# Two transitions of a residual layer: the second norm's root taken from three sums instead of from the updated x

## The reference, cut to what matters

```python
def rmsnorm_2(x, g):
    y = x * lax.rsqrt(jnp.mean(x * x, axis=-1, keepdims=True) + NORM_EPS)
    return y * g

# per layer l; y is what the mixer's last product (conv_out_w or attn_o_w) gives
x = x + g_m[:, None, :] * rmsnorm_2(y, norm_g[l, 1])
h = modulate(rmsnorm_2(x, norm_g[l, 2]), sh_f, sc_f)      # h * (1 + scale) + shift
y = squared_relu_mlp(h, mlp_up_w[l], mlp_down_w[l])
x = x + g_f[:, None, :] * rmsnorm_2(y, norm_g[l, 3])
```

## Time and profile before

| | |
|---|---|
| median of 3 runs | 1802.6 us (1801.67 to 1802.96) |
| the profiled execution | 1802.32 us, its span 1800.5 us |
| PE busy | 1771.8 us of the span (98%) |
| DVE busy | 1069.8 us (59%) |
| ACT busy | 614.2 us (34%) |
| POOL busy | 80.4 us (4%) |
| moved | 215.85 MB, 120 GB/s |

### The profile page before, as it was taken

One profiled execution on the slowest core, in us unless ns is written; L12 is line 12 of the kernel. 1 busy time (PEld: TensorE's weight loads), 2 busy tenths in 40 slices (PEclk: granted clock), 3 DMA queues, 4 the chain that ended last, 5 costly groups with the idle time before them and its releaser, 6 DMA issues. The chain is left out here.

```text
span 1800.5 us, 22782 instructions
## 1 busy us (share of the span) xinstructions
PE 1771.8 (98%) x8216; PEld 1427.2 (79%) x8216; DVE 1069.8 (59%) x1553; ACT 614.2 (34%) x951; POOL 80.4 (4%) x133
## 2 busy tenths in 40 slices
PE   9999999999999999999999999999999999999996
PEld 7777677888888888887888888877767788888885
DVE  5586555655555576776656565657776655434354
ACT  4226444322222343223414232425344342323230
POOL 0000000000000000001000010010000100000001
PEclk9999999999999999999999999999999999999998
DMA  6231112444454434552355555521321134323221
GB/s 230 81 107 36 48 48 60 156 159 152 140 173 146 142 100 132 184 188 94 94 185 181 206 190 184 182 75 59 106 71 60 47 108 161 105 94 96 91 81 47
DMA packets 60127, 215.85 MB, mean 120 GB/s; under 512 B 6672, under 2 KB 6800, under 8 KB 59920
## 3 DMA queue, kind: packets, MB, share of 16 engines
q1 hardware_dynamic: 43632, 154.95, 25.4%
q0 software_dynamic: 16272, 59.25, 10.6%
q10 hardware_dynamic: 144, 0.59, 0.1%
HBM read 212.67 MB, written 2.10 MB: 119 GB/s over the span
## 5 line engine op out<-in xcount | busy, mean ns | idle before, releaser
L707 ACT ACTIVATE w_hi<-w_raw 128x1024 fp32r<-128x1024 f32 x285 | 300.2, 1054 | 458.8 <-PE psum L1623 416.4
L1621 PE MATMUL psum<-h_hi,w_hi 128*128 128x512 f32 x1080 | 421.3, 390 | 1.1 <-DVE h_lo L1057 0.9
L1622 PE MATMUL psum<-h_lo,w_hi 128*128 128x512 f32 x1080 | 420.2, 389 | 0.0
L1623 PE MATMUL psum<-h_hi,w_lo 128*128 128x512 f32 x1080 | 420.2, 389 | 0.0
L1030 DVE TENSOR_TENSOR w_lo<-w_raw,w_hi 128x1024 fp32r<-128x1024 f32 x285 | 348.5, 1223 | 114.1 <-ACT w_hi L707 104.1
L1621 PE MATMUL psum<-hid_hi,w_hi 128*128 128x512 f32 x760 | 295.6, 389 | 0.0
L1622 PE MATMUL psum<-hid_lo,w_hi 128*128 128x512 f32 x760 | 295.6, 389 | 0.0
L1623 PE MATMUL psum<-hid_hi,w_lo 128*128 128x512 f32 x760 | 295.6, 389 | 0.0
L1621 PEld LDWEIGHTS psum<-h_hi,w_hi 128*128 128x128 f32 x1080 | 202.7, 188 | 45.0 <-DVE h_lo L1057 1.3
L1622 PEld LDWEIGHTS psum<-h_lo,w_hi 128*128 128x128 f32 x1080 | 202.7, 188 | 42.2 <-issue 0.5
L1623 PEld LDWEIGHTS psum<-h_hi,w_lo 128*128 128x128 f32 x1080 | 202.7, 188 | 42.0
(11 more groups left out here) (274 smaller groups left out, 1906.7 us busy)
## 6 DMA issues: line engine op xcount, KB each, us to landing
w_raw<-in_wstream SPq DMA_DIRECT2D x285, 512.0 KB, 3.6
ada_raw<-in_ada POOLq DMA_DIRECT2D x112, 512.0 KB, 3.8
x<-in_xT SPq DMA_DIRECT2D x8, 256.0 KB, 6.9
outT<-x SPq DMA_DIRECT2D x8, 256.0 KB, 2.1
con<-in_consts SPq DMA_DIRECT2D x1, 1028.0 KB, 10.6
con<-in_rope ACTq DMA_DIRECT2D x1, 576.0 KB, 5.4
c_row<-in_crow POOLq DMA_DIRECT2D x1, 512.0 KB, 3.9
par<-in_params SPq DMA_DIRECT2D x1, 255.0 KB, 2.7
```

Source lines behind the costliest of these rows:

```text
L707: act.activation(w_hi[:, slot, :], w_raw[:, slot, :], ACT.Copy).then_inc(whi_done, 1)
L1621: pe.matmul(bank, w_hi[:, slot, w], hi[:, ra + k, :], start=k == 0, stop=False)
L1622: pe.matmul(bank, w_hi[:, slot, w], lo[:, ra + k, :], start=False, stop=False)
L1623: mm = pe.matmul(bank, w_lo[:, slot, w], hi[:, ra + k, :], start=False, stop=k == nk - 1)
```

## The change

The two transitions after a mixer (r_m0, r_m1) no longer use `close` and `norm`; the one after the MLP and the last update stay. Since mean(x'^2) = mean(x^2) + 2 r1 mean(x g y) + r1^2 mean((g y)^2), the second root can be had from three means that don't need r1.

- In the last product (`fore=`), after DVE's copy of a chunk to y, ACT squares y and g y, and DVE makes x g y and adds up the three. The sum of y^2 in `ss` takes chunks 0 to 6; chunk 7's squares go into the mean as a matmul of their own.
- Mean of x^2: for r_m0, ACT squares the eight chunks of x, and DVE adds them, in the last six blocks of the convolution's input product (`square_x`); for r_m1 it is the mean that the transition before had made anyway, copied by ACT into `x_mean` (`keep`). To make room, one row of `ada` moves from that stage and four from the output product to the twelve blocks in front.
- Stage `sums`: PE makes the means, then 18 short matmuls (NEW_WARM). Stage `rstd` (first): Ln, Exp, and a copy of the root to PSUM. Stage `resum`: DVE puts the mean of x'^2 together in five instructions, and begins the update. Stage `rstd` (second): Ln and Exp. Stage `renew`: DVE makes the steps r1 g y in place in y, POOL adds chunks 1 to 7 to x (DVE adds chunk 0), and DVE and ACT make h from each chunk.
- In the last step of the product ACT and DVE split one more block of weights (n+4), which the next product's first step then doesn't (`presplit=1`).

```diff
-    def close(gain, middle, end):
+    def renew(old, name, shift, inst):
+        add("sums", dict(aux=1), inst=inst)
+        rstd(EPS2, first_of=inst + 1)
+        add("resum", inst=inst, old=old)
+        rstd(EPS2, second_of=inst + 1)
+        r0 = counts["rhs"]
+        add("renew", dict(val=DT, hi=DT, rhs=DT, xup=1, xpool=DT - 1), inst=inst, old=old, gain=name, shift=shift)
+        return r0
+
+    def close(gain, middle, end, keep=False):
...
-    gemm("conv", 12, "h", h, f0=2, rows=10, scale_x=True)
-    gemm("conv", 6, "h", h, f0=6, rows=6)
+    gemm("conv", 12, "h", h, f0=2, rows=15, scale_x=True)
+    gemm("conv", 6, "h", h, f0=6, rows=5, square_x=True)
     take("g_f0", "r_f0")
-    gemm("acc", 8, "hid", hid, dst="y", first=True, sq=True, rows=4)
-    close("r_m0", 19, 15)
-    h = norm("h", gain="g_f0", shift=24)
+    gemm("acc", 8, "hid", hid, dst="y", first=True, sq=True, fore=0, old="r_m0")
+    h = renew("r_m0", "g_f0", 24, 0)
...
-            gemm("relu2", 8, "h", h, kouter=AHEAD if g == 0 else 0, rows=up[g])
+            gemm("relu2", 8, "h", h, kouter=AHEAD if g == 0 else 0, presplit=1 if g == 0 else 0, rows=up[g])
...
-    close("r_f0", 21, 16)
+    close("r_f0", 21, 16, keep=True)
...
-    gemm("acc", 8, "h", mix, dst="y", first=True, sq=True, kouter=2, begun=6,
+    gemm("acc", 8, "h", mix, dst="y", first=True, sq=True, fore=1, old="r_m1", kouter=2, begun=6,
          turn=-counts["o"] % BANKS)
-    close("r_m1", 19, 15)
-    h = norm("h", gain="g_f1", shift=88)
+    h = renew("r_m1", "g_f1", 88, 1)
...
+        root_wide, mean_g, root_new, mean_mul = psum[:, PT_BANK, :], psum[:, PT_BANK + 1, :], psum[:, PT_BANK + 1, :], psum[:, O_BANK, :]
+        def new_val(c):
+            return psum[:, (O_BANK, AUX_BANK)[c % 2], :]
...
# GpSimd
+                if s["kind"] == "renew":
+                    for c in range(1, DT):
+                        pool.wait_ge(held_done, DT * s["inst"] + c + 1)
+                        pool.tensor_tensor(x[:, c, :], x[:, c, :], y[:, c, :], ALU.add).then_inc(x_pool, 1)
...
# ScalarE, in a step of the last product
+                    if "fore" in s:
+                        c, inst = t.b, s["fore"]
+                        if c == DT - 1:
+                            n = t.n + AHEAD + 1
+                            split_hi(n // RAW + 1, n % SPLIT, t.o + 1)
...
+                        act.activation(y_sq[c % 2], y[:, c, :], ACT.Square).then_inc(y_squared, 1)
...
+                        act.activation(g_sq[c % 2], y[:, c, :], ACT.Square, scale=gain_of(s["old"], c)).then_inc(g_squared, 1)
...
+                elif kind == "rstd" and s.get("first_of"):
+                    act.wait_ge(aux_done, s["at"]["aux"])
+                    act.activation(rstd[:, :], psum[:, AUX_BANK, :], ACT.Ln, bias=eps[s["eps"]][:, :]).then_inc(ln_done, 1)
+                    act.wait_ge(ln_done, s["at"]["rstd"] + 1)
+                    act.activation(rstd[:, :], rstd[:, :], ACT.Exp, scale=-0.5).then_inc(rstd_done, 1)
+                    act.wait_ge(rstd_done, s["at"]["rstd"] + 1)
+                    act.activation(root_wide, rstd[:, :], ACT.Copy).then_inc(root_done, 1)
+                elif kind == "rstd" and s.get("second_of"):
+                    act.wait_ge(resum_done, s["second_of"])
+                    act.activation(resum, resum, ACT.Ln, bias=eps[s["eps"]][:, :]).then_inc(ln_done, 1)
+                    act.wait_ge(ln_done, s["at"]["rstd"] + 1)
+                    act.activation(root_new, resum, ACT.Exp, scale=-0.5).then_inc(rstd_done, 1)
+                elif kind == "renew":
+                    for c in range(DT):
+                        act.wait_ge(val_done, s["at"]["val"] + c + 1)
+                        act.activation(h_hi[:, c, :], new_val(c), ACT.Identity,
+                                       bias=mod[:, s["shift"] + c:s["shift"] + c + 1]).then_inc(hi_done, 1)
...
+                    if s.get("keep"):
+                        act.activation(x_mean[:, :], psum[:, AUX_BANK, :], ACT.Copy).then_inc(mean_kept, 1)
...
# VectorE, in a step of the last product (fore_sums adds y^2 and (g y)^2, add_mul adds x g y)
+                    elif evac == "acc" and "fore" in s:
+                        c, inst = t.b, s["fore"]
+                        if c >= 2:
+                            fore_sums(inst, c - 1)
+                        split_lo(t.n + AHEAD, (t.n0 + AHEAD) % SPLIT)
+                        dve.wait_ge(out_done, t.o + 1)
+                        dve.tensor_copy(y[:, c, :], bank).then_inc(bank_free, 1)
+                        dve.wait_ge(bank_free, BANKS + t.o + 1)
+                        dve.scalar_tensor_tensor(out=y_mul[c % 2], in0=y[:, c, :], scalar=gain_of(s["old"], c),
+                                                 in1=x[:, c, :], op0=ALU.mult, op1=ALU.mult).then_inc(mul_done, 1)
+                        if c >= 1:
+                            add_mul(inst, c)
+                        if c == DT - 1:
+                            n = t.n + AHEAD + 1
+                            split_lo(n, n % SPLIT)
...
+            def new_step(s, c):
+                dve.scalar_tensor_tensor(out=y[:, c, :], in0=y[:, c, :], scalar=gain_of(s["old"], c), in1=root_wide,
+                                         op0=ALU.mult, op1=ALU.mult).then_inc(held_done, 1)
+
+            def resummed(s):
+                dve.wait_ge(means_done, 3 * inst + 1)
+                dve.tensor_tensor(resum, mean_g, rstd[:, :], ALU.mult).then_inc(resum_step, 1)
...
+                dve.scalar_tensor_tensor(out=resum, in0=mean_mul, scalar=2.0, in1=resum, op0=ALU.mult, op1=ALU.add)\
+                   .then_inc(resum_step, 1)
...
+                dve.tensor_tensor(resum, resum, rstd[:, :], ALU.mult).then_inc(resum_step, 1)
...
+                    dve.tensor_tensor(resum, resum, psum[:, AUX_BANK, :], ALU.add).then_inc(resum_step, 1)
...
+                dve.tensor_scalar(resum, resum, 0.0, None, ALU.max).then_inc(resum_done, 1)
+                dve.wait_ge(root_done, inst + 1)
+                new_step(s, 0)
+                dve.wait_ge(held_done, DT * inst + 1)
+                dve.tensor_tensor(x[:, 0, :], x[:, 0, :], y[:, 0, :], ALU.add).then_inc(x_done, 1)
+                new_step(s, 1)
+
+            def renew(s):
...
+                for c in range(DT - 2):
+                    val(c)
+                    new_step(s, c + 2)
+                    low(c)
+                val(DT - 2)
+                val(DT - 1)
+                low(DT - 2)
+                low(DT - 1)
...
# TensorE
+                elif kind == "sums":
+                    pe.matmul(psum[:, AUX_BANK, :], mean[1024][:, :], ss[:, :], start=True, stop=False)
+                    pe.matmul(mean_g, mean[1024][:, :], g_sum, start=True, stop=False)
+                    pe.matmul(psum[:, AUX_BANK, :], mean[1024][:, :], y_sq[1], start=False, stop=True).then_inc(aux_done, 1)
+                    pe.matmul(mean_g, mean[1024][:, :], g_sq[1], start=False, stop=True).then_inc(means_done, 1)
+                    pe.matmul(mean_mul, mean[1024][:, :], mul_sum, start=True, stop=True).then_inc(means_done, 1)
+                    if inst == 0:
+                        pe.wait_ge(ln_done, s["at"]["rstd"] + 1)
+                        pe.matmul(psum[:, AUX_BANK, :], mean[1024][:, :], x_sum, start=True, stop=True).then_inc(means_done, 1)
+                    keep_warm(NEW_WARM, next(p for p in PLAN[idx:] if p["kind"] == "gemm")["at"]["o"] % BANKS)
```

More of the change, by code:

```diff
@@ L49 @@
 WARM_START, WARM = 28, 9
+NEW_WARM = 18
 SHIFT = 1
@@ L89, in gemm @@
         about["h0"] = hi_of[r0]
-        if evac == "acc" and about.get("sq"):
+        if evac == "acc" and about.get("sq") and "fore" not in about:
             inc.update(sqv=nblk, ss=nblk + (0 if about.get("more") else 1) - (0 if about.get("go_on") else 1))
@@ L326, in steps @@
     turns = nblk // body
-    first = 1 if stage["at"]["n"] == 0 or done else 0
+    first = 1 if stage["at"]["n"] == 0 or done or stage.get("presplit") else 0
     if last:
@@ L1094, in gemm @@
                 more = s.get("more", False)
-                if evac == "acc" and s["sq"] and not more:
+                if evac == "acc" and s["sq"] and not more and "fore" not in s:
                     dve.memset(ss[:, :], 0.0).then_inc(ss_done, 1)
@@ L1111, in step @@
                                or isinstance(t.b, int) and t.b < s.get("presplit", 0))
-                    if not nothing and not s.get("late") and not s.get("twin"):
+                    if not nothing and not s.get("late") and not s.get("twin") and "fore" not in s:
                         split_lo(t.n + AHEAD, (t.n0 + AHEAD) % SPLIT)
```

99 lines of the change are left out of this document (93 added, 6 removed).

## The result

The changed kernel takes 1792.11 us (median of 5 runs, 1791.66 to 1794.0) against 1802.6 (1801.53 to 1803.18): the ratio of the runs is 0.9946, 95% interval 0.9935 to 0.9956, so 7.9 to 11.7 us are gone. The forecast was 1793.2, range 1790.8 to 1797.2. The profiled execution has a span (first to last instruction) of 1790.3 us, 10.2 less than before.

A forecast was written before the change was run, and what follows sets the result against it. The prediction took the serial chain in two transitions, about 18.1 us each without useful PE work, as the bound. Gains of 2 x 4.68 = 9.4 us off 1802.32 gave 1792.9, or 1793.2 beside the median, range 1790.8 to 1797.2.

The forecast's parts named there:

- What bounds the kernel: Two transitions: each costs about 18.1 us in which PE makes nothing the next product needs, set by the serial chain.
- First root: In each transition, after the last copy: Ln at 2.85 us, Exp 0.71 later, DVE starts at 4.38, before 4.23.
- T: The moment at which DVE can copy the output product's last block, 834.77 us in the first transition before the change.
- Chain: DVE's mean of x'^2 and update start: dependent instructions 0.73 to 0.79 apart, first value of h at 10.22 us.
- The rule of the Trainium skill on chained Vector instructions: Semaphores cost nothing extra; by it five links are 0.6 us shorter per transition, time 1792.0; forecast followed the rows instead.
- The turn: DVE's three instructions per chunk of h, with a wait for ACT: 2.29 us a chunk, over PE's 2.04, six chunks.
- GpSimd: POOL's adds to x in the two transitions take 1.29 us each and hold up no value; nothing lost.
- Rival 1: PE's clock falls in the gap before the first chunk, then returns: 1793 to 1797, say 1795 us; chance 0.18.
- Rival 2: Lower clock stays through the next product's first chunks: each transition 10.2 us later than before, 1822 us; chance 0.05.
- Rivals 3 and 4: 3: turn longer than 2.29, 1796.6 to 1800.3 us, chance 0.08; 4: DVE late to last copy, 1797.7, chance 0.04.
- Sum: Two transitions gaining 4.68 us each, 9.4 off the profiled 1802.32: 1792.9, or 1793.2 beside the median.

The follow-up runs named there:

- kernel with the gap filled: 28 and 32 short matmuls instead of 18 in the first and third transitions, against the changed kernel; median 1793.33 us against 1792.72 on the same chip.

## Why the prediction was right, point by point

- **What bounds the kernel.** Right: 9.1 of the 10.2 us by which the spans differ lie between the last copy and the first relu of two transitions.
- **First root.** Ln came 2.86 after T (836.75; forecast 2.85), Exp 3.57 (3.56); DVE began at 4.48 (4.38). The row names PE's L2112 as what ended DVE's wait, but by the program L1402 needs only the root and the mean before it (L2110); the Exp ended at 838.09, 0.28 ahead. The other means were in time: L2112 ended at 838.36, 0.81 ahead of the second instruction, and L2116 at 839.22, 1.40 ahead of the fourth.
- **Chain.** 0.72 to 0.80 apart; I had one link of 0.79, but it is the first and not the one behind the scalar_tensor_tensor, and no run tells why. The last instruction takes 0.43 instead of 0.49. The start of two stages cost 0.39 where I had taken 0.30. First value at T + 10.31 (10.22), first matmul at 11.99 (11.93).
- **The rule of the Trainium skill on chained Vector instructions** ("VectorE: DVE Perf Modes", section "The DRAIN you can't avoid"), by which a semaphore between them costs nothing extra: the trace after disagrees again. L1408 starts 0.73 and L1412 0.72 behind their forerunners of 0.69, with a semaphore between, while DVE's next step of y, which doesn't need the value in front of it, starts 0.67 behind that one of 0.76 (844.20, 844.87).
- **The turn.** 2.17 us instead of 2.29. ACT begins h_hi 0.78 behind the start of the value, not 0.85 (846.44 and 847.22; only the first chunk has 0.85), its pass takes 0.69, not 0.73, and the low part follows a little sooner. By my sum with 2.17 the relu would be at 29.0; the runs at full clock have 28.9.
- **GpSimd.** Right: its adds take 1.26 to 1.30 us (1.29 forecast), and no value waits for one.
- **Rival 1 happened, at less than its price.** The granted clock fell in both transitions of the profiled execution. I had given it 0.18, and had called its first 3 us free because PE had 0.25 us a chunk in hand. With the shorter turn it has only 0.13 in hand, and the fall cost 0.9 a transition (29.82 against 28.92). The two errors, of turn and of clock, cancel: 29.68 forecast, 29.82 found. So the number was right partly by luck, with one mechanism in it that I held for unlikely. By my own sign ("I am wrong if a stretch behind a transition shows 0.50") the forecast's course of events was wrong in this step, though the gain itself came from where I had put it.
- **Rival 2** (the clock stays): not in any trace. Even after 6.66 and 7.52 us of idleness it came back while the product ran. By its own terms its price is 1822.7 (1802.3 + 2 x 10.2), not 1822. The Trainium skill, "TensorE: Matmul & The Clock Gate", section "Part 1: The HAM clock gate", says that activity releases the lower clock. No row of before showed it; the trace without short matmuls agrees (0.50 until 849.40, 0.95 in the 2.6 us behind it).
- **Rivals 3 and 4**: the turn was shorter, and DVE was waiting for the last copy by 0.89 to 0.90 us in both products (0.95 forecast). In the attention's product the first copy that waits for PE so long again is the seventh of eight, so DVE had caught up one step ahead of T.
- **Sum.** 9.1 us in the transitions (9.4 forecast); the medians differ by 10.5, within an interval of 7.9 to 11.7. Of the two first traces the rest is the opening (0.85) and the 0.28 of the second transition, and neither has the fall at 102 us. For the medians the rest isn't resolved.

What stays open: how often the clock falls in each gap, since nine gaps with seven falls are few, and what else than the gap decides it. The kernel with the gap filled shows what the falls cost in the trace, but not in its own median. Nor does any run part the gain of the early second root from that of taking the eight squares and their matmuls off the path: both edits are one change here.

## What to carry to other kernels

When a reduction stands between two dependent norms, its second result can often be had from sums over what is known before the first, gathered while the matmul engine still works; the price is on engines with time to spare. After shortening such a chain, look at what the short filler matmuls must now cover, since the chain's engine and the matmul engine's clock limit the same stage by turns, and an edit to one shows only with the other. And where two executions of one program differ by 0.1%, look for the granted clock in thin stretches far from the change before giving a difference to the edit.

## What the runs showed of the hardware that I had not expected

- Rows that show PE busy are no proof that its clock holds: behind 28 matmul rows of the forget gates' sums, twenty of them eight columns wide, with no idle time, it was at 0.50 in six traces and at 1.00 in five.
- Behind the same gap of 2.6 us the clock held in two traces and fell in three, behind one of 3.5 us it fell in all four; with 0.4 us of idleness or less it fell in none of the ten gaps of the five traces in which the gap is filled.
- Where DVE sets the pace, a fall costs less than half of its length: 0.9 us for 3.4 at half clock, 1.8 for 6.8, and 1.3 and 2.2 where part of it lay in the idle time itself. At 102 us, where PE has work without a gap, it costs about half, 1.7 us for 3.4.
